# Two units of each projection start on the scaled residual, before its norm is known

## What is computed

```python
def rms_norm(x, g):
    y = xf * lax.rsqrt(jnp.mean(xf * xf, axis=-1, keepdims=True) + EPS)
    return (y * g).astype(x.dtype)

def modulate(h, shift, scale):
    return h * (1 + scale) + shift

h = modulate(rms_norm(x, norm_g[i, 0]), sh0, sc0)
x = x + 0.5 * g0 * swiglu(h, ffn_w_gu[i, 0], ffn_w_down[i, 0])
```

## Time and profile before

| | |
|---|---|
| Median of three runs | 2856.43 us (2852.49 to 2859.24) |
| Span of the profiled execution, its own time | 2868.0 us |
| TensorE busy (matmuls) | 2783.2 us, 97% |
| VectorE busy | 1428.6 us, 50% |
| ScalarE busy | 979.6 us, 34% |
| GpSimd busy | 241.9 us, 8% |
| Chain that ended last, TensorE's share | 91% |
| Mean granted TensorE clock | 0.986 of full |

### The profile page before, as it was taken

One profiled execution on the slowest core, in us unless ns is written; L12 is line 12 of the kernel. 1 busy time (PEld: TensorE's weight loads), 2 busy tenths in 40 slices (PEclk: granted clock), 3 DMA queues, 4 the chain that ended last, 5 costly groups with the idle time before them and its releaser, 6 DMA issues.

```text
span 2868.0 us, 40754 instructions
## 1 busy us (share of the span) xinstructions
PE 2783.2 (97%) x16211; PEld 2249.2 (78%) x16211; DVE 1428.6 (50%) x2059; ACT 979.6 (34%) x1530; POOL 241.9 (8%) x318
## 2 busy tenths in 40 slices
PE   8999888999999999999989999999999999999998
PEld 7855777887887878888878888788887866788887
DVE  4588643666776455555443332433324876433322
ACT  3355443333332232222342222322223265422222
POOL 1000110112000111001110000100002300100000
PEclk8899999999999999999999999999999999999999
DMA  6331001673332655566323333233333310233332
GB/s 234 115 99 59 3 3 32 218 229 118 102 93 87 204 152 195 186 199 197 100 68 95 95 95 98 88 95 95 92 101 97 108 37 23 77 100 95 93 94 70
DMA packets 89844, 311.07 MB, mean 108 GB/s; under 512 B 11632, under 2 KB 12400, under 8 KB 89584
## 3 DMA queue, kind: packets, MB, share of 16 engines
q1 hardware_dynamic: 66928, 232.62, 26.0%
q0 software_dynamic: 22784, 76.56, 8.7%
HBM read 305.99 MB, written 2.10 MB: 107 GB/s over the span
## 4 chain that ended last, share of the span: by engine, by line
PE 91%; DVE 4%; ACT 3%; issue 1%; POOL 1%; DMA 1%; SPq 0%; DVEq 0%; ACTq 0%; POOLq 0%
PE psum L1924 24%; PE psum L1926 24%; PE psum L1925 24%; PE psum L2101 1%; PE psum L2103 1%; PE psum L2102 1%; PE psum L2612 1%; PE psum L2601 1%; PE psum L1999 1%; PE psum L1995 1%; PE psum L1996 1%; PE psum L2303 1%; PE psum L2076 1%; PE psum L2392 1%; PE psum L2273 1%
## 5 line engine op out<-in xcount | busy, mean ns | idle before, releaser
L1144 DVE TENSOR_TENSOR w_lo<-stage,w_hi 128x1024 fp32r<-128x1024 f32 (+2 forms) x441 | 518.3, 1175 | 827.4 <-ACT w_hi L655 827.2
L655 ACT ACTIVATE w_hi<-stage 128x1024 fp32r<-128x1024 f32 (+2 forms) x441 | 449.7, 1020 | 1206.1 <-PE psum L1926 1171.7
L1924 PE MATMUL psum<-h_hi,w_hi 128*128 128x512 f32 (+1 forms) x2024 | 792.7, 392 | 3.3 <-DVE w_lo L1144 2.3
L1925 PE MATMUL psum<-h_lo,w_hi 128*128 128x512 f32 (+1 forms) x2024 | 790.9, 391 | 0.0
L1926 PE MATMUL psum<-h_hi,w_lo 128*128 128x512 f32 (+1 forms) x2024 | 790.5, 391 | 0.0
L1924 PEld LDWEIGHTS psum<-h_hi,w_hi 128*128 128x128 f32 (+1 forms) x2024 | 381.1, 188 | 86.7 <-DVE w_lo L1144 4.4
L1926 PEld LDWEIGHTS psum<-h_hi,w_lo 128*128 128x128 f32 (+1 forms) x2024 | 381.0, 188 | 80.2
L1925 PEld LDWEIGHTS psum<-h_lo,w_hi 128*128 128x128 f32 (+1 forms) x2024 | 381.1, 188 | 79.6
L1924 PE MATMUL psum<-hid_hi,w_hi 128*128 128x512 f32 x880 | 344.0, 391 | 6.5 <-DVE hid L1234 6.5
L1926 PE MATMUL psum<-hid_hi,w_lo 128*128 128x512 f32 x880 | 343.4, 390 | 0.0
L1925 PE MATMUL psum<-hid_lo,w_hi 128*128 128x512 f32 x880 | 343.2, 390 | 0.0
(11 more groups left out here) (440 smaller groups left out, 3023.0 us busy)
## 6 DMA issues: line engine op xcount, KB each, us to landing
stage<-in_up SPq DMA_DIRECT2D x220, 512.0 KB, 3.6
mod_w<-in_mod_w POOLq DMA_DIRECT2D x144, 512.0 KB, 4.3
stage<-in_down SPq DMA_DIRECT2D x80, 448.0 KB, 3.3
stage<-in_down SPq DMA_DIRECT2D x40, 512.0 KB, 3.5
stage<-in_w_in SPq DMA_DIRECT2D x24, 512.0 KB, 3.6
stage<-in_w_qkv SPq DMA_DIRECT2D x24, 512.0 KB, 3.6
stage<-in_w_merge SPq DMA_DIRECT2D x16, 512.0 KB, 4.5
turned_n<-in_cmp_w SPq DMA_DIRECT2D x1, 4096.0 KB, 13.1
```

The source lines that it names most:

```text
L655: act.activation(w_hi[:, c % 2, 0:kt * cols], stage[:, c % NSTAGE, 0:kt * cols], ACT.Copy).then_inc(hi_done, 1)
L1144: dve.tensor_tensor(w_lo[:, c % 2, 0:kt * cols], stage[:, c % NSTAGE, 0:kt * cols], w_hi[:, c % 2, 0:kt * cols].bitcast(F32), ALU.subtract ...
L1924: pe.matmul(dst, wh[:, n], a_hi[:, k], start=start and n == 0, stop=False)
L1925: pe.matmul(dst, wh[:, n], a_lo[:, k], start=False, stop=False)
```

## The change

For norms 1, 2, 4, 5, 6 and 7 (`EARLY`) the first two units behind the norm no longer multiply `h`. ScalarE forms `u_hi`, the rounded scaled residual, right after each square (`early_hi`), VectorE its rest (`early_lo`), and `early_units` multiplies these as soon as TensorE is through with the segment before; the second unit runs EARLY_LAG = 4 tiles behind. `u` lies in `h_hi` and `h_lo` (for norm 7 in `qk_hi` and `qk_lo`). The sums of squares and the spread stand inside this stream, after its steps 0, 2 and 4, and these norms lose their `keep_busy`. Where there is a shift, each k tile also gets two matmuls with two columns, the shift split in two. Once the normal path of the norm is through, VectorE copies the spread factor from bank 5 to SBUF, adds up the shift's columns, and multiplies both banks by the factor (`early_products`). The third unit is an ordinary one that now waits k by k.

Below, `early_hi` and `round_h` run on ScalarE, `early_units` and the last `down` on TensorE, and the rest on VectorE.

```diff
+EARLY_LAG = 4
+EARLY = (1, 2, 4, 5, 6, 7)
...
-        MOD_AT = {"mix_in": 0, "merge": 25, "mix_out": 57, "down0": 64, "up1": 85, "down1": 129}
+        MOD_AT = {"mix_in": 0, "merge": 25, "mix_out": 65, "down0": 72, "up1": 93, "down1": 137}
...
+            def early_hi(n_norm, k):
+                act.wait_ge(x_ready, KD * NORM[n_norm] + k + 1)
+                act.activation(early_of(n_norm)[0][:, k], xT[:, k], ACT.Copy, scale=SCALE[n_norm][k]).then_inc(uhi_done, 1)
...
             def round_h(n_norm, shift, also={}, first=0):
                     act.wait_ge(t_done, at + 1)
+                    if n_norm in EARLY and k < KD - 1:
+                        act.wait_ge(u_used, (KD - 1) * early_before(n_norm) + k + 1)
+                    elif n_norm in EARLY:
+                        act.wait_ge(unit_done, first + 2)
...
+            def early_products(n_norm, first, tile, dst):
+                if n_norm > 1:
+                    dve.tensor_reduce(shift_w[:], psum[:, 6, 0:4]..., AX.X, ALU.add).then_inc(early_step, 1)
+                for e in range(2):
+                    dve.tensor_tensor(dst[e], bank(tile + e), bc_of[n_norm], ALU.mult).then_inc(early_step, 1)
...
             def spread(n_norm):
                 dve.reciprocal(rstd[:], std[:]).then_inc(rstd_done, 1)
+                early_lo(n_norm, KD - 1)
...
             def norm(...):
+                if n_norm in EARLY:
+                    dve.tensor_copy(bc_of[n_norm], psum[:, 5, :]).then_inc(early_copy, 1)
...
             def body(i):
+                        if early:
+                            early_products(...)
+                        else:
+                            lo(c + 2, i)
...
+                        if early and f:
+                            dve.scalar_tensor_tensor(out=hid[:, q], in0=taps[:, 1], scalar=shift_w[:, 1:2], in1=s_buf[:, q],
+                                                     op0=ALU.add, op1=ALU.mult).then_inc(hid_done, 1)
...
-                        mod(MOD_AT["merge"] + 4 * n + j)
+                        mod(MOD_AT["merge"] + 5 * n + j)
+                        if j == 3:
+                            mod(MOD_AT["merge"] + 5 * n + 4)
...
+            def early_units(s, n_norm):
+                for step in range(KD + EARLY_LAG):
+                    for e, at in ((0, step), (1, step - EARLY_LAG)):
...
+                    if step in (0, 2):
+                        sum_early(n_norm, step == 2)
+                    if step == 4:
+                        spread_rstd(n_norm)
...
             def down(f, n_norm):
-                        pe.wait_ge(hid_done, pairs + KF)
+                        pe.wait_ge(hid_done, pairs + KF - 1 + n // 2)
```

More of the change, by code:

```diff
@@ L687, in _, with round_h @@
             shifts = [0]
-            def round_h(n_norm, shift, also={}):
+            def early_hi(n_norm, k):
+                if n_norm not in EARLY:
+                    return
+                if n_norm > 1 and k == 0:
+                    act.wait_ge(mod_vec, 1 if n_norm < 5 else 2)
+                act.wait_ge(x_ready, KD * NORM[n_norm] + k + 1)
+                act.activation(early_of(n_norm)[0][:, k], xT[:, k], ACT.Copy, scale=SCALE[n_norm][k]).then_inc(uhi_done, 1)
+            def round_h(n_norm, shift, also={}, first=0):
                 for k in range(KD):
@@ L708, in body @@
                         p = pairs + 2 * i + q
-                        hi(s.first + 2 * q + 2, i)
+                        early = isinstance(i, int) and i == 0 and q == 0
+                        if not early:
+                            hi(s.first + 2 * q + 2, i)
                         if f == 0:
@@ L1028, in _ @@
                     hi(1)
-                act.wait_ge(mod_vec, 1)
-                round_h(2, shift(0, 0))
+                round_h(2, shift(0, 0), {4: (seg["up1"].first + 2,)}, seg["up1"].first)
                 up(1)
@@ L1046, in _ @@
                     square(4, n)
+                    early_hi(4, n)
                 root(4)
-                round_h(4, shift(0, 2))
+                round_h(4, shift(0, 2), {4: (seg["up2"].first + 2,)}, seg["up2"].first)
                 up(2)
@@ L1226, in body @@
                         p, c = pairs + 2 * i + q, s.first + 2 * q
-                        lo(c + 2, i)
+                        early = isinstance(i, int) and i == 0 and q == 0
+                        if early:
+                            early_products(UP_NORM[f], s.first, s.tile,
+                                           (s_buf[:, 1], hid[:, 0]) if f == 0 else (taps[:, 0], taps[:, 1]))
+                        else:
+                            lo(c + 2, i)
                         if f == 0:
@@ L1759, in _ @@
                 dve.wait_ge(mod_vec, 1)
-                norm(2, scale(0, 0), shift(0, 0))
+                norm(2, scale(0, 0), shift(0, 0), {5: (seg["up1"].first + 2,)})
                 up(1)
-                down(1, gate(0, 0))
+                down(1, gate(0, 0), 3)
                 s = seg["pool"]
@@ L1776, in _ @@
                                              op0=ALU.mult, op1=ALU.add).then_inc(x_ready, 1)
-                norm(4, scale(0, 2), shift(0, 2))
+                    if n >= 1:
+                        early_lo(4, n - 1)
+                norm(4, scale(0, 2), shift(0, 2), {5: (seg["up2"].first + 2,)})
                 up(2)
-                down(2, gate(0, 2))
                 if first_block:
@@ L1815, in raw_of_v @@
                     dve.tensor_copy(raw_v[:, h % 2], psum[:, 5, :]).then_inc(raw_done, 1)
+                early_products(6, s.first, s.tile, (raw[:, 0], raw[:, 1]))
+                for n in range(2):
+                    dve.wait_ge(early_step, steps_before(6) + 2 + n)
+                    dve.tensor_scalar(raw[:, n], raw[:, n], shift_w[:, n:n + 1], None, ALU.add).then_inc(raw_done, 1)
                 for n in range(2 * KD):
@@ L1914, in _, with product @@
         def _(pe):
-            def product(c, i, k_tiles, acts, tile, start, stop):
+            def product(c, i, k_tiles, acts, tile, start, stop, n_norm=None):
                 c, i = fixed(c, i)
@@ L1933, in keep_busy, with sum_early @@
                         pe.matmul(psum[:, 7, at:at + 256], ident, cst[:, 0:256], start=True, stop=True)
+            def sum_early(n_norm, last):
+                src = sq(n_norm, KD - 1) if last else sq_sum
+                if last:
+                    pe.wait_ge(sq_done, KD * NORM[n_norm] + KD)
+                else:
+                    pe.wait_ge(acc_done, adds_before(n_norm) + ADDS)
+                for tt in range(TT):
+                    m = pe.matmul(psum[:, 4, tt:tt + 1], src[:, tt * P:(tt + 1) * P], means[:, 0:1],
+                                  start=not last and tt == 0, stop=last, skip_group_check=True)
+                if last:
+                    m.then_inc(ssq_done, 1)
             def sum_squares(n_norm, k):
+                if n_norm in EARLY:
+                    return
                 def over_tokens(src, start, stop):
@@ L1974, in body @@
                             if j == 0:
-                                first_units(s, n_norm)
+                                early_units(s, n_norm)
                         else:
-                            product(s.first + j, i, range(KD), (h_hi, h_lo), s.tile + j, True, True)
+                            product(s.first + j, i, range(KD), (h_hi, h_lo), s.tile + j, True, True,
+                                    n_norm if isinstance(i, int) and i == 0 and j == 2 else None)
                 for start, count in UP_RUNS[f]:
@@ L2584, in _ @@
                     if n == 0:
[L2585 removed]
+                        early_units(s, 6)
                     elif n >= 2:
[L2587 removed]
+                        product(s.first + n, 0, range(KD), (h_hi, h_lo), s.tile + n, True, True, 6 if n == 2 else None)
                 for part in range(4):
```

161 lines of the change are left out of this document (119 added, 42 removed).

## The result

| | before | after |
|---|---|---|
| Median of the runs | 2855.58 us (2852.49 to 2859.24, 4 runs) | 2899.68 us (2897.22 to 2901.49, 4 runs) |
| Ratio, 95% interval | | 1.014 [1.0114, 1.0167] |
| Span of the profiled execution | 2868.0 us | 2895.5 us |

A forecast was written before the change was run, and what follows sets the result against it. With TensorE busy 97%, only its waits and vain work could be won. Losses at the norms, `merge` and 8.5 of clock, less 9.5 at the downs, made +14.1 us: 2870.5 us on the median, range 2852 to 2884.

The forecast's parts named there:

- `merge`, y_lo: In `merge`, the fifth condition product waits for its load, so y_lo comes 3.7 us later with nothing covering it.
- norm 1: At norm 1, a queued condition product slows each tile; fourth unit done at 34.9 against 31.4, +3.5 us.
- norm 2: At norm 2, a condition product in `up1` between `hid` and w_lo adds 0.8; +1.6 us, idle 2.8.
- norm 4: At norm 4, GpSimd's chain of adds starts 0.7 later and slow clock also slows useful work; +1.0 us.
- norm 5: At norm 5, the fourth unit starts at 26.0 and ends at 31.5, before at 30.7; 0.8 us worse.
- norm 6: At norm 6, shift additions stand ahead of GpSimd's swap; fifth unit ends at 39.8 instead of 36.1, +3.7 us.
- downs: Each `down` no longer waits for the last hidden tile; 9.5 us off, including 1.7 of slow clock at `down0`.
- clock: 1.7 us for each new wait near 3 us or more: merge, two at norm 1, norms 2 and 6; 8.5 in all.
- What bounds the kernel now: Whole kernel: TensorE is busy 97%, so only its waits or vain work can be won; six norms put 53 us in play.
- the rival of the slots: In `merge`, landings of 5.0 us make five products need 17.3 us against a tile's 16.5; +6, 2877, chance 0.15.
- 21.55: At norm 5, when the norm ends on VectorE; the steps behind it bring the fourth unit's w_lo to 26.0.
- a sign of being wrong: In the changed kernel's trace, short matmuls less than 0.05 us apart were to show the forecast wrong.

The follow-up runs named there:

- e3: Kernel before with only the weaker wait of the first tiles of each down (21 hidden tiles, not 22); median 2858.8 us, ratio 0.9993.
- e10: Early units at norms 5 and 7 only, fourth w_lo first, short matmuls last, placement restored, four condition products per merge tile, e3's wait; 2845.02 us.
- e2: Changed kernel with its pad APART smaller by 104 floats, so hid, o and y lie where they lay before; 2879.29 us, ratio 1.008.
- e1: Kernel before with only an unused pad of 416 bytes per partition where the change has its shift tensors; 2883.27 us, ratio 1.0096.
- e4: e2 with four condition products to an output tile of merge again, the vectors for norm 2 formed ahead of down0; 2872.2 us, ratio 1.006.
- e6: e2 without 28 of the 32 two-column matmuls at each of five norms; 2878.22 us, ratio 1.006.
- e11: Changed kernel with e2 and e4, fourth unit's w_lo first, two-column matmuls behind each unit's last product; 2857.43 us, ratio 1.0.

## Why the prediction was wrong, step by step

From the first product of `merge` on, without clock except in its own line; a norm's value is what its segment is longer than in e3, which has the new wait at the downs too; norm 6 has the attention behind it in it:

| step | forecast | measured |
|---|---|---|
| place of hid, o, y | none | +21.7 |
| `merge`, y_lo | +3.7 | +7.7 |
| norm 1 | +3.5 | +1.8 |
| norm 2 | +1.6 | +2.1 |
| norm 4 | +1.0 | +4.4 |
| norm 5 | +0.8 | +1.1 |
| norm 6 | +3.7 | +3.3 |
| norm 7 | +0.8 | +1.2 |
| downs (1.7 of clock set apart) | -7.8 | -8.9 |
| clock | +6.8 | +8.5 |
| sum | +14.1 | +42.9 |

The split between norm 1 and the downs hangs on e3's slow clock behind norm 1; with the 3.3 of e10 ahead of `down0` it is +1.0 and -8.1.

- **The missing term.** "What bounds the kernel now" took 0.227 us for a product as given. The change's part list named every instruction and not one allocation, though the change allocates `shift_2`, and a pad of 376 floats in front of hid asks what it is for. 21.7 is 5 x 4.0 in the downs (against e2) and 1.7 in `merge` and `mix_out` (as in e1). Without it the kernel would stand 21 us behind, and e2 does stand inside the range at 2879.3 us; but the other terms are not right for that, they add up to 21 where 14 was forecast, and the next two make up that difference.
- **"There y_lo now comes 3.7 us later and nothing covers it"** was mis-sized. The terms given for it, a wait of 1.7 and a product of 1.22, make 2.9 and not 3.7, and the wait for y_lo grew from 0.5 to 2.9 us; but the loads of mod_w held VectorE up in earlier tiles too, and TensorE paid at w_lo. This is the rival of the slots, in part; the two are not alternatives but add up. e4, which takes the fifth product out, gives back all of e2's 6.9 in `merge` and `mix_out`.
- **Norm 4, "a slow clock that now also slows useful work: +1.0"**: the mechanism was right, its size not. Behind the wait for GpSimd's adds TensorE runs at half clock, and five groups of products now lie there, between the sums and the spread; at half clock a group takes 1.7 us. At full clock it takes 0.92, so the slow clock alone costs five groups 3.9 us. From the first sums to the spread it takes 11.7 us, where it took 6.1 before. No run sets this term apart from the others at norm 4.

```profile
1454.87 1.87 PE L2051 MATMUL psum<-cst,rexp 128*128 128x1 f32 x8 [2.63 <-POOL rexp L585]
...
1466.59 1.06 PE L2084 MATMUL psum<-cst,rstd 128*128 128x128 f32 x8
```

```profile
1456.00:1458.00 2.00, 2.00 (x8) 1.83 (x9) 0.00 (x0) 0.00 (x0) 0.00 (x0) 0.50 0.00 0
...
1464.00:1466.00 2.00, 2.00 (x6) 1.71 (x7) 0.00 (x0) 0.00 (x0) 0.00 (x0) 0.50 0.00 0
```

- **Right**: norms 5, 6, 7 and 2 within about half a microsecond; the chain through the copy, the reduction and the products, though the terms listed for it behind 21.55 make 25.7 and not 26.0; and a group of 0.92 us. Two short matmuls add 0.23 us to a group, 0.115 each, and e6 puts them at 12 us of the whole. Between the two the recorded starts are often only 0.03 us apart, which the prediction had named as a sign of being wrong; the next product then starts 0.11 later and the one after it 0.31 later, so that sign misleads. The Trainium skill's 25 ns (TensorE: Matmul & The Clock Gate, "Wait — 56ns, not 53.3ns?") agrees with that one distance, but it is not what a short matmul with its own 128-column weights costs here.

```profile
1839.40 0.16 PE L2129 MATMUL psum<-shift,w_hi 128*128 128x2 f32 x1
1839.43 0.25 PE L2131 MATMUL psum<-shift,w_lo 128*128 128x2 f32 x1
1839.54 0.48 PE L2133 MATMUL psum<-h_hi,w_hi 128*128 128x512 f32 x1
1839.85 0.39 PE L2134 MATMUL psum<-h_hi,w_lo 128*128 128x512 f32 x1
```

- **Norm 1** came out better than its +3.5: the sums waited 1.9 (3.0 in e2) and the fourth unit 5.4, against 3.3 and 6.3.

```profile
667.43 1.05 PE L2051 MATMUL psum<-cst,rexp 128*128 128x1 f32 x8 [1.93 <-POOL rexp L585]
```

- **The clock**: each drop cost 1.7 us or a multiple of it in the tally. Against before there is one after the 2.9 us at y_lo, two behind norm 1, one each behind norms 2 and 6 and one more in the attention, which I had not counted; the one at `down0` went, and norm 4 keeps its 8.5. The windows in and behind norm 1's wait for the fourth unit:

```profile
690.00:692.00 2.00, 0.00 (x0) 0.00 (x0) 1.97 (x3) 0.88 (x3) 0.00 (x0) 0.82 0.00 0
692.00:694.00 2.00, 1.45 (x4) 1.17 (x5) 2.00 (x3) 0.97 (x2) 0.00 (x0) 0.50 0.33 35
694.00:696.00 2.00, 2.00 (x6) 1.61 (x5) 1.93 (x4) 0.00 (x0) 0.00 (x0) 0.50 0.78 260
696.00:698.00 2.00, 2.00 (x6) 1.52 (x6) 0.46 (x1) 0.63 (x1) 0.00 (x0) 0.50 0.64 211
698.00:700.00 2.00, 2.00 (x10) 1.66 (x9) 0.00 (x0) 0.00 (x0) 0.00 (x0) 0.98 0.05 18
```

## What to carry to other kernels

When a diff allocates anything, list what is allocated behind it and compare addresses before pricing instructions; a pad with an odd number in the source may mark a place that was tuned, as it did here. Work that is put ahead of a chain shortens the end only if the chain's own start does not move back with it: here the spread of the factor started 3.7 us later (7.3 in place of 3.6), and at norm 5 the fourth unit came 0.8 us later by the forecast and the segment 1.1 longer by the trace. When a median hides a step of a few microseconds, read it segment by segment in the trace, with the clock's loss set apart.

## What the runs showed of the hardware

A 128x512 product whose moving operand lay 416 bytes off the weights' and h's place took 397 ns in place of 389 and followed the one before after 0.2343 us in place of 0.2267; 32 bytes off 396, 128 off 393, and 256, 512 or 1024 off no slower. In e11 the early products of norm 7 with qk_hi and w_lo, where qk_hi lies 192 bytes past a multiple of 256 from h's place by the program's addresses, took 394 ns, and the same line with h_hi 389. The loss at 416 bytes is 3.3% of TensorE's time in such products, and neither the busy share (97% both times) nor the list of waits shows it.
